# Loading the first half of x in two column parts, in a two-layer encoder kernel on one core

## The chip, the cores and the metric

The kernel runs on one NeuronCore of a Trainium2 chip. The engines are TensorE (PE in the rows; its weight loads are PEld), VectorE (DVE), ScalarE (ACT), GpSimd (POOL) and SyncE (SP), which here only issues DMA transfers. The metric is the device time of one execution in microseconds (us). A lower time is better.

## The reference

The program computes two layers of an encoder over 256 tokens of width 1024, in float32. Cut to what matters:

```
def mixer_sublayer(x, norm_g, w_in, qk_g, rpb, mix_g, w_out):
    h = rms_norm(x, norm_g)
    proj = h @ w_in                                  # 256 x 1024 @ 1024 x 2304
    qa, ka, va, qb, kb, vb, qc, kc, vc = jnp.split(proj, ...)
    ...                                              # three kinds of attention: oa, ob, oc
    merged = jnp.concatenate([rms_norm(oa, ...), rms_norm(ob, ...), rms_norm(oc, ...)], axis=-1)
    return merged @ w_out

for l in range(2):
    x = x + mixer_sublayer(x, norm1_g[l], w_in[l], ...)
    x = x + hier_moe(rms_norm(x, norm2_g[l]), ...)   # 32 experts, two of them per token
```

`rms_norm(x, g)` divides each row of x by the root of its mean square and multiplies by a gain per column.

## The kernel before, in words

Each layer has two stages. In the mixer stage the input projection `w_in` comes in three groups of 768 columns (C, A, B, in this order), and attention is interleaved with them. In the expert stage the 32 experts' weights (6 MB each) stream through a ring of 16 pieces of 1 MB in SBUF, with some further buffers beside it. All engines run a program that is written out by hand: each engine's instructions stand in the order of the code, and engines wait for each other by semaphores only.

The change is at the very start of layer 0. The 256 tokens are two halves of 128 rows (`t` = 0 and 1), which lie in SBUF as `x[:, t]`, 128 partitions of 1024 columns. Every projection needs x turned, with its columns on the partitions. TensorE turns it in blocks of 128 columns: `half_turned(l, t, j)` turns four blocks, columns 512 j to 512 j + 511 of half t, into one PSUM bank. VectorE multiplies these by the gain of `norm1_g` into `hT` (`rows_turned`, line 1439). The projection uses the turned x as its weights (`project`, line 782). The division by the row's root is done later, when VectorE takes a projection out of PSUM (`projected`, line 1453): ScalarE sums the squares (`x_squares` and `mean_squares`, line 1212), GpSimd takes the root (lines 661 and 664).

SyncE's queue starts like this (`mixers`, lines 526 to 557): the identity matrix `ident` (64 KB), x's first half (512 KB, one transfer, semaphore `d_x[0]`), the upper four row blocks of the first 256 columns of group C (512 KB, semaphore `landed`), x's second half (512 KB, `d_x[1]`), the lower four row blocks of these columns (512 KB, `d_lower[0]`), and then the other 512 columns of group C in two transfers of 1 MB. Behind them come the window biases (`in_na_rpb`, `in_c_flip`), the rotary tables (`in_c_rope`), the gains of queries and keys (`in_qk_norm_g`, line 470), a mask, group A (line 562), and so on without a wait until the expert stage's first pieces. Three small transfers of gains (4 KB each) are issued from ScalarE's own queue (line 1308, semaphore `d_gains`).

TensorE starts like this (its `mixers`): it waits for `ident`, runs two warming products of the identity (line 741), waits for the gains and turns them (line 791), and then

```
                if l == 0:
                    half_turned(l, 0, 0)
                half_turned(l, 0, 1)
                project(l, 0)
                project(l, 1)
                project(l, 2)
```

In `project(l, 0)`, between block 3 and block 4, x's second half is turned as well.

Of the kernel before, what the change touches and what calls it, by code (L numbers as in the profile page):

```python
# [163 lines left out]
def encoder(nc, a, out):  # L164
    ctx = ExitStack()
    with ctx:
        def sb(name, shape, dt=F32):
            return ctx.enter_context(nc.sbuf_tensor(name, shape, dt))

        def sem(name):  # L170
            return ctx.enter_context(nc.semaphore(name))
# [3 lines left out]
        x = sb("x", [P, TT, D])  # L175
# [87 lines left out]
        def carve(n):  # L263
# [32 lines left out]


        d_x = [sem(f"d_x{t}") for t in range(TT)]
        d_ident, d_gains, d_rel, d_mask, d_rope, d_qkg, d_route, d_gain2, d_const, d_out = (
            sem("d_" + n) for n in ("ident", "gains", "rel", "mask", "rope", "qkg", "route", "gain2", "const", "out"))  # L300

# [117 lines left out]
        def _(sp):  # L419
            extra = sp.alloc_register("sp_extra")  # L420
            xr = a["x"].rearrange("b (t p) d -> (b p) t d", t=TT)
# [104 lines left out]
            def mixers(l):  # L526
                if l == 0:
                    sp.dma_start(ident[:], a["c_ident"]).then_inc(d_ident, 16)
                    sp.dma_start(x[:, 0], xr[:, 0]).then_inc(d_x[0], 16)
                for g in range(3):  # L530
                    if g == 1:
                        if l == 0:
# [96 lines left out]
            def rerun(l, j, x0):  # L629
# [3 lines left out]
                for r in range(6):  # L633
                    w, k = weight(("w_gate", "w_up", "w_down")[r // 2], l, bass.ds(expert, 1))
                    sp.dma_start(rows(r, k), w[:, 0, r % 2 * k:r % 2 * k + k]).then_inc(d_again, 16)

            run_layers(sp, extra, mixers, first, item, rerun, seen[0])

            outr = out.rearrange("b (t p) d -> (b p) t d", t=TT)
# [93 lines left out]
        def _(pe):  # L733
# [13 lines left out]
            def half_turned(l, t, j):  # L747

                if l == 0:
                    pe.wait_ge(d_x[t], 16)  # L750
                else:
                    pe.wait_ge(v_back[BACK.index((t, j))], l)
                for k in range(4):
                    last = transpose(bank[2 * t + j][:, k * P:k * P + P], x[:, t, (4 * j + k) * P:(4 * j + k + 1) * P], ident[:])
                last.then_inc(p_xT, 1)
# [177 lines left out]
            def mixers(l):  # L933
# [3 lines left out]
                if l == 0:  # L937
                    half_turned(l, 0, 0)
# [265 lines left out]
        def _(act):  # L1204
# [6 lines left out]
            def mean_squares(t, c):  # L1211
                activation(h[:, t * D:t * D + D], x[:, t, :], ACT.Square, scale=D ** -0.5, accum_out=ms[:, c:c + 1]).then_inc(a_ms, 1)  # L1212

            def x_squares(l, t):
                if l == 0:
                    act.wait_ge(d_x[t], 16)
                else:
                    for half in range(2):
                        act.wait_ge(v_back[BACK.index((t, half))], l)
                mean_squares(t, t)  # L1220
# [89 lines left out]
            def mixers(l):  # L1310
                if l == 0:
                    first_loads()
                    act.wait_ge(g_init, 4)
                x_squares(l, 0)
                x_squares(l, 1)

                activation(spare[:], one[:], ACT.Exp)
# [640 lines left out]
```

## Time and profile before

| | us |
|---|---|
| median of 3 runs | 1154.4 |
| lowest and highest of them | 1153.38, 1154.82 |
| the profiled execution | 1152.95 |
| its span, from the first to the last instruction | 1151.1 |
| TensorE busy in it | 981.2 |
| VectorE, ScalarE, GpSimd busy | 291.6, 178.2, 51.6 |
| DMA, over the span | 437.08 MB, mean 380 GB/s |

The profile is of one execution. Its time is the span and 1.85 us around it. All times within it are counted from the start of the span. "SPq" and "ACTq" are the DMA issues of SyncE and ScalarE; the time of an issue is that of issuing alone, and the time to landing is told apart from it.

### The profile page before, as it was taken

How to read it: one execution, taken by the hardware profiler on the slowest of the kernel's cores; microseconds unless marked ns; L12 is line 12 of the kernel's file. 1: busy time of each engine (PE TensorE's matmuls, PEld its weight loads, DVE VectorE, ACT ScalarE, POOL GpSimd, SP SyncE). 2: the span in 40 equal slices, each digit the busy share in tenths (PEclk: the TensorE clock that was granted, in tenths of full speed). 3: DMA queues.
4: the chain of work that ended last, by engine and by line, in shares of the span. 5: the costliest groups of instructions: out<-in, count | busy, mean ns of one | idle time of the engine just before them, and what ended most of it. 6: DMA issues, size and time to landing. Idle time of an engine off the chain costs nothing.

```text
span 1151.1 us, 13649 instructions
## 1 busy us (share of the span) xinstructions
PE 981.2 (85%) x5406; PEld 461.6 (40%) x5406; DVE 291.6 (25%) x796; ACT 178.2 (15%) x444; POOL 51.6 (4%) x104
## 2 busy tenths in 40 slices
PE   8999999998887956548899999999969879484687
PEld 5556644453343412114356656444524334131232
DVE  4546552111110110001145555421111101100011
ACT  1344311110010000002024343111100001000110
POOL 2121100000000000000021211000000000000000
PEclk9999999999898977869999999999989989687899
DMA  9962989999999999999998248999999999999997
GB/s 318 345 259 110 363 317 422 424 427 428 428 428 427 428 430 426 429 428 421 400 396 319 101 178 342 358 419 427 428 428 427 428 428 427 428 427 428 428 420 299
DMA packets 64759, 437.08 MB, mean 380 GB/s; under 512 B 11229, under 2 KB 15669, under 8 KB 34229
## 3 DMA queue, kind: packets, MB, share of 16 engines
q1 hardware_dynamic: 64645, 436.16, 92.4%
q8 instruction: 45, 0.74, 0.3%
q14 instruction: 21, 0.17, 0.0%
q10 hardware_dynamic: 48, 0.01, 0.0%
HBM read 435.10 MB, written 1.44 MB: 379 GB/s over the span
## 4 chain that ended last, share of the span: by engine, by line
PE 63%; DMA 31%; DVE 3%; SPq 1%; issue 1%; POOL 1%; ACT 0%; DVEq 0%; POOLq 0%
PE bank L1071 32%; DMA ring<-in_w_down 16%; DMA ring<-in_w_gate 10%; PE bank L782 9%; DMA ring<-in_w_up 5%; PE bank L1097 5%; PE bank L914 5%; PE bank L1025 4%; PE bank L741 1%; PE bank L860 1%; PE bank L850 1%; SPq L513 1%; PE bank L882 1%; PE bank L1089 1%; PE bank L873 1%
## 5 line engine op out<-in xcount | busy, mean ns | idle before, releaser
L1071 PE MATMUL bank<-ring,work 128*32 128x512 f32 (+2 forms) x2608 | 480.8, 661 | 133.7 <-DMA ring<-in_w_up 50.5
L1071 PEld LDWEIGHTS bank<-ring,work 128*32 128x32 f32 (+2 forms) x2608 | 145.3, 129 | 397.7 <-issue 394.5
L782 PE MATMUL bank<-ring,hT 128*128 128x512 f32 (+1 forms) x384 | 128.3, 488 | 0.9 <-DVE hT L1439 0.8
L782 PEld LDWEIGHTS bank<-ring,hT 128*128 128x128 f32 x384 | 71.2, 190 | 48.1 <-issue 42.2
L1025 PEld LDWEIGHTS bank<-work,h 128*128 128x128 f32 x704 | 82.3, 192 | 16.5 <-issue 15.6
L1025 PE MATMUL bank<-work,h 128*128 128x128 f32 x704 | 86.8, 277 | 1.6 <-DVE work L1804 1.6
L1071 PE MATMUL bank<-work 128*32 128x512 f32 (+2 forms) x176 | 75.1, 617 | 13.8 <-DMA ring<-in_w_down 13.8
L1097 PE MATMUL bank<-work 128*128 128x512 f32 x176 | 81.4, 603 | 2.4 <-ACT work L1392 1.6
L1071 PE MATMUL bank<-kept,work 128*32 128x512 f32 (+1 forms) x160 | 72.6, 606 | 4.2 <-DMA ring<-in_w_up 4.2
L1860 DVE COPY work<-bank 128x512 f32<-128x512 f32 x20 | 13.8, 692 | 243.6 <-PE bank L1071 243.6
L1855 DVE TENSOR_TENSOR work<-work,bank 128x512 f32<-128x512 f32 x22 | 15.1, 688 | 218.3 <-PE bank L1071 218.3
L1826 DVE TENSOR_SCALAR work<-iota,work,rstd 128x128 f32<-128x128 f32 x80 | 22.3, 343 | 185.2 <-PE bank L1119 183.6
L914 PE MATMUL bank<-ring,h 128*128 128x512 f32 x128 | 58.2, 600 | 0.0
L1387 ACT COPY work<-bank 128x512 f32<-128x512 f32 x22 | 12.9, 585 | 269.5 <-PE bank L1144 269.5
L1383 ACT COPY work<-bank 128x256 f32<-128x256 f32 x22 | 8.2, 372 | 297.4 <-PE bank L1119 297.4
L1097 PEld LDWEIGHTS bank<-work 128*128 128x128 f32 x176 | 31.8, 189 | 50.9 <-issue 49.2
L1392 ACT COPY work<-bank 128x512 f32<-128x512 f32 x22 | 12.9, 585 | 170.7 <-PE bank L1071 156.2
L1071 PEld LDWEIGHTS bank<-work 128*32 128x32 f32 (+2 forms) x176 | 21.2, 135 | 39.4 <-issue 39.2
L741 PE MATMUL bank<-ident 128*128 128x384 f32 x86 | 31.8, 514 | 2.8 <-DMA ident<-in_c_ident 2.8
L914 PEld LDWEIGHTS bank<-ring,h 128*128 128x128 f32 x128 | 23.2, 190 | 25.3 <-issue 25.0
L1372 ACT ACTIVATE work<-bank,gain 128x128 f32<-128x128 f32 x88 | 25.1, 368 | 42.1 <-PE bank L1025 42.1
L661 POOL TENSOR_TENSOR ms<-ms,eps 128x1 f32<-128x1 f32 x20 | 3.8, 189 | 552.0 <-ACT h L1212 466.0
(212 smaller groups left out, 716.8 us busy)
## 6 DMA issues: line engine op xcount, KB each, us to landing
ring<-in_w_gate SPq DMA_DIRECT2D x42, 2048.0 KB, 25.1
ring<-in_w_down SPq DMA_DIRECT2D x38, 2048.0 KB, 23.8
ring<-in_w_up SPq DMA_DIRECT2D x36, 2048.0 KB, 30.0
ring<-in_w_up SPq DMA_DIRECT2D x36, 1024.0 KB, 14.7
ring<-in_w_down SPq DMA_DIRECT2D x28, 1024.0 KB, 10.3
ring<-in_w_gate SPq DMA_DIRECT2D x20, 1024.0 KB, 8.1
ring<-in_w_in SPq DMA_DIRECT2D x8, 1536.0 KB, 13.6
ring<-in_w_out SPq DMA_DIRECT2D x8, 1024.0 KB, 17.0
```

What stands on the lines that cost most here:

```text
L741: matmul(bank[b][:, 0:3 * P].rearrange("p (n s) -> p n s", n=3), ident[:], ident[:].unsqueeze(1).broadcast_to([P, 3, P]), start=True, stop ...
L782: last = matmul(bank[6 + i % 2][:, 0:c1 - c0], hT[:, k, t * P:t * P + P], group_in(l, gi)[:, k, c0:c1], start=(k == 0), stop=(k == KD - 1))
L914: last = matmul(bank[6 + n % 2][:, :], mixed[:, pos0 + c, t * P:t * P + P], rows(pos, 2)[:, c % 2, half * 512:half * 512 + 512], start=(c ...
L1025: last = nc.tensor.matmul(bank[banks[k // 4]][:, k % 4 * P:k % 4 * P + P], x_kc[:, t, k, :], pick[:, t, :], start=(t == 0), stop=(t == TT ...
L1071: last = nc.tensor.matmul(bank[b][e * w:e * w + w, :], lhs[:, k, e * w:e * w + w], rows(pos, k_count // 2)[:, kk, n * 512:n * 512 + 512], ...
L1097: last = nc.tensor.matmul(bank[SUM0 + n][:, :], pickT[:, t, :], y[:, half * 512:half * 512 + 512], start=(of == 0), stop=(of == NI - 1))
L1372: last = nc.scalar.mul(xg[:, k, :], bank[pair(i)[1]][:, (k - 4) * P:(k - 3) * P], gain2[:, q // NI, k:k + 1])
L1387: nc.scalar.copy(hidT.rearrange("p c s -> p (c s)"), bank[b0][:, :]).then_inc(a_hidT, 1)
L1392: nc.scalar.copy(y[:, 0:512], bank[b0][:, :]).then_inc(a_y, 1)
L1826: last = ts(hot[:, n], iota[:, 0:P], seats[:, TIME[i], n:n + 1], factors[n], ALU.is_equal, ALU.mult)
L1855: tt(hid, hid, bank[b1][:, :], ALU.mult).then_inc(v_hid, 1)
L1860: nc.vector.tensor_copy(y[:, 512:1024], bank[b1][:, :]).then_inc(v_y, 1)
```

## The change

The load of x's first half becomes two transfers, of columns 0 to 511 and of columns 512 to 1023, each 128 rows of 2 KB (256 KB). The first one raises `d_x[0]`, the second a new semaphore, `d_right`. TensorE's first turn (columns 0 to 511) waits for `d_x[0]`, the second turn for `d_right`. ScalarE, which squares all 1024 columns of the half, waits for both. Nothing else is edited.

```
+        d_right = sem("d_right")
...
                     sp.dma_start(ident[:], a["c_ident"]).then_inc(d_ident, 16)
-                    sp.dma_start(x[:, 0], xr[:, 0]).then_inc(d_x[0], 16)
+                    for j in range(2):
+                        sp.dma_start(x[:, 0, j * 512:j * 512 + 512], xr[:, 0, j * 512:j * 512 + 512]).then_inc((d_x[0], d_right)[j], 16)
...
             def half_turned(l, t, j):
                 if l == 0:
-                    pe.wait_ge(d_x[t], 16)
+                    pe.wait_ge(d_right if (t, j) == (0, 1) else d_x[t], 16)
...
             def x_squares(l, t):
                 if l == 0:
                     act.wait_ge(d_x[t], 16)
+                    if t == 0:
+                        act.wait_ge(d_right, 16)
```

On SyncE, at the start of the program, the queue of transfers before was this:

```order
L528 DMA ident<-in_c_ident 128x128
L529 DMA x<-in_x 128x1024
L555 DMA ring<-in_w_in 128x4x256
L557 DMA x<-in_x 128x1024
L555 DMA ring<-in_w_in 128x4x256
L555 DMA ring<-in_w_in 128x4x512 x2
```

And with the change (the lines are numbered one or two higher):

```order
L529 DMA ident<-in_c_ident 128x128
L531 DMA x<-in_x 128x512 x2
L557 DMA ring<-in_w_in 128x4x256
L559 DMA x<-in_x 128x1024
L557 DMA ring<-in_w_in 128x4x256
L557 DMA ring<-in_w_in 128x4x512 x2
```

Everything behind x's first half stands one issue later; the order is the same.

On TensorE, at the start of the program, with the semaphores it waits for, before:

```order
L741 MATMUL bank<-ident 128x384 [waits d_ident]
L741 MATMUL bank<-ident 128x384
L791 MATMUL bank<-ident,work 128x24 [waits d_gains]
L754 MATMUL bank<-ident,x 128x128 [waits d_x0]
L754 MATMUL bank<-ident,x 128x128 x3
L754 MATMUL bank<-ident,x 128x128 [waits d_x0]
L754 MATMUL bank<-ident,x 128x128 x3
L782 MATMUL bank<-ring,hT 128x256 [waits landed0,v_xT]
```

And with the change:

```order
L743 MATMUL bank<-ident 128x384 [waits d_ident]
L743 MATMUL bank<-ident 128x384
L793 MATMUL bank<-ident,work 128x24 [waits d_gains]
L756 MATMUL bank<-ident,x 128x128 [waits d_x0]
L756 MATMUL bank<-ident,x 128x128 x3
L756 MATMUL bank<-ident,x 128x128 [waits d_right]
L756 MATMUL bank<-ident,x 128x128 x3
L784 MATMUL bank<-ring,hT 128x256 [waits landed0,v_xT]
```

No instruction moved; the fifth turn waits for another semaphore.

## Rows read from the trace of the kernel before

**Rows 1.** Busy us by stretch (PE, PEld, DVE, ACT, POOL), granted clock, DMA share, GB/s
```profile
0.00:30.00 30.00, 27.10 (x99) 16.21 (x100) 12.72 (x29) 5.68 (x10) 7.61 (x23) 1.00 0.93 305
...
86.00:115.00 29.00, 28.21 (x143) 17.58 (x142) 19.55 (x44) 12.15 (x43) 4.42 (x9) 1.00 0.28 109
```

**Rows 2.** Chain of waits, the first 11 us: start, duration, what
```profile
0.78 1.91 DMA ident<-in_c_ident
...
2.80 2.90 PE bank L741 x4
5.70 0.23 PE bank L791
5.93 1.06 PE bank L754 x4
...
7.84 1.99 PE bank L782 x8
9.83 0.87 PE bank L754 x8
```

**Rows 3.** Timeline of TensorE's matmuls and weight loads, three places: start, duration, what
```profile
4.86 0.85 PE L741 MATMUL bank<-ident 128*128 128x384 f32 x1
...
5.63 0.18 PEld L791 LDWEIGHTS bank<-ident,work 24*128 24x128 f32 x1 [1.08 <-DMA work<-in_norm_g]
...
6.77 0.66 PEld L754 LDWEIGHTS bank<-ident,x 128*128 128x128 f32 x3
...
10.44 0.52 PEld L782 LDWEIGHTS bank<-ring,hT 128*128 128x128 f32 x3
```

**Rows 4.** Timeline, SyncE's issues from 1.2 to 2.8 us: start, duration of the issue
```profile
1.22 0.42 SPq L529 DMA_DIRECT2D x<-in_x  x1
1.69 0.43 SPq L555 DMA_DIRECT2D ring<-in_w_in  x1
2.16 0.51 SPq L557 DMA_DIRECT2D x<-in_x  x1
2.71 1.93 SPq L555 DMA_DIRECT2D ring<-in_w_in  x3
```

**Rows 5.** Issues by line, four short windows: KB each, us from issue to landing
```profile
x<-in_x SPq DMA_DIRECT2D x1, 512.0 KB, 4.1
...
ring<-in_w_in SPq DMA_DIRECT2D x1, 512.0 KB, 5.1
...
x<-in_x SPq DMA_DIRECT2D x1, 512.0 KB, 5.9
...
ring<-in_w_in SPq DMA_DIRECT2D x1, 1024.0 KB, 9.1
ring<-in_w_in SPq DMA_DIRECT2D x1, 512.0 KB, 6.9
```

**Rows 6.** DMA packets of 5.0 to 5.2 us, then of 5.6 to 6.0 us
```profile
DMA packets 72, 0.07 MB, mean 369 GB/s; under 512 B 0, under 2 KB 72, under 8 KB 72
...
DMA packets 118, 0.17 MB, mean 420 GB/s; under 512 B 8, under 2 KB 100, under 8 KB 118
```

**Rows 7.** Timeline, 5 to 16 us, of ScalarE, GpSimd and VectorE
```profile
5.40 1.28 ACT L1212 ACT_TABLE_LOAD   x1 [5.40 <-DMA x<-in_x]
...
8.26 0.55 POOL L664 TENSOR_TENSOR rstd<-ms,mhalf 128x1 f32<-128x1 f32 x1
...
12.47 0.48 DVE L1453 TENSOR_SCALAR work<-bank,rstd 128x256 f32<-128x256 f32 x1 [0.88 <-PE bank L782]
...
15.93 0.48 DVE L1453 TENSOR_SCALAR work<-bank,rstd 128x256 f32<-128x256 f32 x1 [2.97 <-PE bank L782]
```

**Rows 8.** Timeline, 18 to 26 us, from the scaled rotary table to the turned keys
```profile
18.63 0.46 POOL L689 TENSOR_TENSOR kept<-kept 128x128 f32<-128x128 f32 x1
...
22.29 0.76 DVE L1498 TENSOR_TENSOR work<-work 128x256 f32<-128x256 f32 x2
...
25.41 0.42 PEld L816 LDWEIGHTS bank<-ident,work 128*128 128x128 f32 x4 [0.60 <-issue]
```

More of the change, by code:

```diff
@@ L298, in encoder @@
         d_x = [sem(f"d_x{t}") for t in range(TT)]
+        d_right = sem("d_right")
         d_ident, d_gains, d_rel, d_mask, d_rope, d_qkg, d_route, d_gain2, d_const, d_out = (
@@ L528, in mixers @@
                     sp.dma_start(ident[:], a["c_ident"]).then_inc(d_ident, 16)
-                    sp.dma_start(x[:, 0], xr[:, 0]).then_inc(d_x[0], 16)
+                    for j in range(2):
+                        sp.dma_start(x[:, 0, j * 512:j * 512 + 512], xr[:, 0, j * 512:j * 512 + 512]).then_inc((d_x[0], d_right)[j], 16)
                 for g in range(3):
@@ L749, in half_turned @@
                 if l == 0:
-                    pe.wait_ge(d_x[t], 16)
+                    pe.wait_ge(d_right if (t, j) == (0, 1) else d_x[t], 16)
                 else:
@@ L1216, in x_squares @@
                     act.wait_ge(d_x[t], 16)
+                    if t == 0:
+                        act.wait_ge(d_right, 16)
                 else:
```

## The prediction

> **What bounds the kernel now.** I read the busy time by stretch first, then the chain of waits, then the timeline of the first 16 us, then how long each transfer took to land.
>
> The busy time by stretch [rows 1] says which engine the start hangs on. Of its first 30 us TensorE is busy for 27.1, and the other 2.9 are the wait at the very start. The reader is to see three more things: the granted clock is 1.00, that is the upper of the two levels (2.4 GHz), the DMA engines are busy for 0.93 of this stretch at 305 GB/s, and later in the same mixer stage, from 86 to 115 us, they are busy for 0.28 only. So the start is a matter of TensorE's path, and a transfer that lands somewhat later has room to be caught up before the expert stage begins. A shift of TensorE at the start would on the other hand be passed on to the end, since TensorE has next to no idle time in the mixer stage.
>
> The chain of waits [rows 2] says what TensorE's path is. `ident` is issued at 0.78 and takes 1.91 us. TensorE then runs the two warming products (four instructions, 2.80 to 5.70), the turn of the gains (5.70), the four turns of x's left half (5.93), and after VectorE's product the projection (7.84). No transfer of x is in the chain. That is the main finding: the first turn does not wait for x.
>
> When does x's first half land? Its issue starts at 1.22 [rows 4] and it takes 4.1 us [rows 5], so it lands at 5.3. ScalarE, which really waits for it, starts its table load at 5.40 [rows 7], which agrees. TensorE cannot start a turn before it has done the warming products and the gains: the last warming instruction starts at 4.86, the gains' weight load at 5.63 [rows 3], the first turn at about 5.9. x has been there for some 0.5 us by then.
>
> **The change part by part.**
>
> The first part alone is waited for. x's left half is 256 KB. It cannot land later than the whole did, as it is the first half of the same bytes on the same queue. Its landing goes from 5.3 to, say, 4.6: the 256 KB saved are 0.6 to 0.7 us at the 369 to 420 GB/s that the DMA engines moved at [rows 6]. TensorE is at 4.6 still in its third or fourth warming instruction. Worth: 0. The upper bound on any gain, if x's landing did gate the turn in executions other than the profiled one, is these 0.7 us.
>
> The second part. It is issued one issue later than the left half, at about 1.22 + 0.42 + 0.05 = 1.69. It moves the second half of the same bytes. Earliest landing 5.3 as before, latest 5.3 and one issue, 0.47 us (the distance of the issues at 1.22 and 1.69 [rows 4]), so 5.8. TensorE wants it for the fifth turn, whose weights load at 6.77 [rows 3]. 1.0 us of slack. Cost 0.
>
> More packets. The half now goes as 256 pieces of 2 KB where it was 128 of 4 KB. The trace shows no 2 KB pieces in this stretch, so I bound them by smaller ones: from 5.0 to 5.2 us all 72 packets are under 2 KB (the weights' rows of 1 KB), at 369 GB/s. From 5.6 to 6.0, with larger ones among them, it is 420 GB/s [rows 6]. 512 KB take 1.42 us at the one rate and 1.25 at the other. So the smaller pieces cost between 0 and 0.17 us. I take 0.1 on the DMA engines, and look below whether anything on the path sees it.
>
> Everything behind on SyncE's queue is issued 0.47 us later. That is one more instruction on a queue that doesn't wait before the expert stage. Each of these transfers lands between 0 later (the DMA engines are the limit from 4 us on, and they have the same bytes to move in the same order) and 0.47 + 0.17 = 0.64 us later. I go through the ones that TensorE's path needs early:
> - The upper blocks of the first 256 columns: issue at 1.69, 5.1 us, landed at 6.8 [rows 4, 5]. Used at 7.84 [rows 2]. Slack 1.0.
> - x's second half: 2.16 + 5.9 = 8.1 [rows 4, 5]. Turned from 9.83 on, in the chain [rows 2]. Slack 1.8 (1.4 by the weight load, which runs ahead).
> - The lower blocks: 2.71 + 6.9 = 9.6 [rows 4, 5]. Used from 10.44 on [rows 3]. Slack 0.8. This is the tightest, and still 0.2 above the worst of the two bounds.
> - The next 512 columns, upper blocks: issued about 0.47 behind, at 3.2, 9.1 us, landed at 12.3 [rows 5]. The second unit of the projection is taken out at 15.93 [rows 7], and only then does the third begin. Slack 3.6.
> - The query and key gains, for GpSimd's rotary products at 18.63 [rows 8]. Here GpSimd may start up to 0.64 later, and VectorE with it. VectorE has the keys ready at 22.29 + 0.76 = 23.05, and TensorE takes them at 25.41, after the bias products. Slack 2.4.
> - All others land farther from their use, and before the expert stage there is the stretch at DMA share 0.28 [rows 1], some 20 us of free DMA time. Cost 0 in each.
>
> ScalarE's second wait. Both squares need all of x's first half. ScalarE waits to 5.3 before and to 5.3 to 5.8 now, then loads the table and squares. What is queued behind it is the square of the second half, and GpSimd's two roots wait for these. The first root is there at 8.26 + 0.55 = 8.8, and its first reader, VectorE, comes at 12.47, released by TensorE [rows 7]. Slack 3.7, against a cost of at most 0.64. The second root is a square and a root behind it, and is read at 15.93. Cost 0.
>
> Sum: 0 on TensorE's path. The profiled execution would stay at 1152.95 us (span 1151.1 and 1.85 around it). The median of the runs shown is 1154.4, 1.45 above it. That is the runs' own scatter (1153.38 to 1154.82), so I forecast the median again: 1154.4 us.
>
> One rule speaks against the change. From issue to landing the two 512 KB transfers of 1.22 and 1.69 took 4.1 and 5.1 us, so they landed 1.5 us apart, and the next two followed after 1.3 and 1.5 us [rows 4, 5]. The Trainium skill, page "DMA: Bandwidth & Descriptors", section "Anatomy of one DMA — SWDGE (gpsimd) path", gives every DMA some 2.0 us of fixed time and then its bytes at 436 GB/s, and the same page's section "Measured (HBM→SBUF, 128 partitions, SWDGE, issued from GpSimd)" asks for transfers of 1 MiB and up. By that a half alone would be an estimated 2.6 us, and if the two halves stood one behind the other, x would be there 2 us later than by one transfer, which would make TensorE wait. The trace does not agree that they stand so: 512 KB every 1.3 to 1.5 us is 350 to 400 GB/s, and leaves no room for 2 us of each.
>
> **The rivals.**
>
> A, slower: the transfers of a queue are served with a cost of each that adds up, and the lower weight blocks come too late. Place: TensorE's weight load at 10.44. Nearest row for such a cost: `ident`, 64 KB, 1.91 us from issue to landing [rows 2]. If the extra transfer adds that whole, the lower blocks land at 9.6 + 1.9 = 11.5, and TensorE stands for 1.1 us. It decides from a delay of 0.8 us on. There is a second price: in its first turns TensorE took 1.06 us for four, in the next ones 0.87 for eight [rows 2], 0.27 against 0.11 each, although the granted clock reads 1.00. It had been idle before 2.80 and ran at the slow rate to about 8. If a stop sends it back to that for as long (5.2 us), it loses half of them, 2.6 us. Together 3.7 us, 1158.1. For it: the slack is the smallest here. Against it: landings 1.3 to 1.5 us apart, and that TensorE also waits for VectorE before 7.84 without a slow stretch after it.
>
> B, a little faster: x does gate the first turn in ordinary executions, or the small gain transfers, which share the DMA engines with x, get through earlier. The first is worth up to 0.7 us as above. For the second, the warming instructions are 0.64 apart, so TensorE could have gone on at 4.86 + 0.64 = 5.50, and the gains' load is at 5.63 [rows 3]: 0.13 us. At best 1153.7. For it: the mark at the gains' load names a transfer. Against it: 0.5 us of slack for x in the trace.
>
> C, a little slower: the delay is 0.8 to 1.2 us somewhere without the slow rate after it; up to 0.4 us, 1154.8.
>
> That the change doesn't do what it says is not a rival: the order of SyncE and the waits of TensorE show it. What fails is its effect.
>
> **How the numbers follow.** A measurement of this kernel can tell 0.2%, 2.3 us, from no change. Forecast, no effect: 0.86. B: 0.05. C: 0.03. A: 0.04. The last 0.02 are for a gain that no row shows. B and C are within 0.2%. The runs' scatter alone (1.44 us over three) can put a kernel with no effect past 0.2% in some 2 of 100 cases to either side, half of which I count to each. So faster 0.03, within 0.2% 0.92, slower 0.05. The range holds the scatter of such medians and bends toward A: 1152.2 to 1157.0.
>
> **What would show it.** Right: SyncE issues two transfers of x of 256 KB at 1.2 and 1.7, and all behind them 0.4 to 0.5 us later. The left half lands near 4.6, and TensorE's gains' load and first turn still start at 5.6 and 5.9. The fifth turn is at 6.8, the projection at 7.8, its second half at 10.4, with no DMA named before it. ScalarE's table load starts at 5.3 to 5.8, and VectorE takes the first unit at 12.5. Wrong: a first turn clearly before 5.8 (B), or idle time of TensorE before 10.4 released by `in_w_in` and slow turns after it (A).

## The result, and the profile after

| | before | after |
|---|---|---|
| median, us (20 runs each) | 1153.74 | 1155.46 |
| lowest and highest | 1152.48, 1154.82 | 1153.25, 1158.55 |
| ratio of the medians of both, 95% interval | | 1.0016, 1.0010 to 1.0022 |
| the profiled execution and its span | 1152.95, 1151.1 | 1155.61, 1153.8 |

The change makes the kernel slower by 1.7 us by the medians. It is a small loss, but its interval excludes no change, and the scatter grew: the highest run is 3.7 us above the highest of before. I had forecast no effect, so the forecast was wrong, although 1155.46 lies in its range. The loss is 0.16%, within the 0.2% that my prediction took for the finest difference that a measurement of this kernel can tell; 20 runs of each kernel told it.

The chain of waits of the changed kernel, which is the counterpart of [rows 2], shows how far TensorE is behind. Columns are start, duration, what; the lines of code are numbered two to four higher.

```profile
0.78 1.97 DMA ident<-in_c_ident
...
2.86 2.90 PE bank L743 x4
...
5.99 1.06 PE bank L756 x4
...
7.89 1.99 PE bank L784 x8
9.89 0.48 PE bank L756 x4
...
10.39 0.70 DVE hT L1443
...
11.21 12.28 PE bank L784 x40
...
34.14 6.87 PE bank L784 x16
```

To 7.89 all is within 0.1 us of before, as forecast: the first turn did not wait for x, and the earlier left part bought nothing. The eight instructions at 7.89 are the first half of the first projection, on the upper blocks. Behind them come the turns of x's second half, and then a group of 40 projection instructions, of which the first need the lower blocks. I use the start of this group below to tell how late TensorE is. It begins at 11.21, where it was 10.71 before. This view cuts overlapping instructions differently in the two kernels; by the weight load at the head of the group the shift is 0.74 us (11.18 against 10.44). The unit at 34.14 was at 33.38 in the same view of before: 0.76 us of shift by then.

What held TensorE shows in the transfers. First SyncE's issues (start, duration), the counterpart of [rows 4]:

```profile
1.22 0.90 SPq L531 DMA_DIRECT2D x<-in_x  x2
2.16 0.45 SPq L557 DMA_DIRECT2D ring<-in_w_in  x1
2.65 0.50 SPq L559 DMA_DIRECT2D x<-in_x  x1
3.20 1.72 SPq L557 DMA_DIRECT2D ring<-in_w_in  x3
```

Then the issues by line in short windows (KB each, us from issue to landing), the counterpart of [rows 5]: x's left part, x's second half, the upper blocks and the lower blocks.

```profile
x<-in_x SPq DMA_DIRECT2D x1, 256.0 KB, 3.0
...
x<-in_x SPq DMA_DIRECT2D x1, 512.0 KB, 7.0
...
ring<-in_w_in SPq DMA_DIRECT2D x1, 512.0 KB, 5.4
...
ring<-in_w_in SPq DMA_DIRECT2D x1, 512.0 KB, 7.9
```

Issue and time to landing add up to the landing: left part 4.2 (x was at 5.3 as a whole), upper blocks 7.6 (6.8 before), x's second half 9.6 (8.1), lower blocks 11.1 (9.6). The issues are 0.47 later, as forecast, but the last two landings are 1.5 later. The lower blocks were wanted at 10.44, and the 40 instructions start just behind their landing. The second half was wanted at 9.46 by the weight load that runs ahead. The rows of the two weight loads, first that of the second half's turns, then that of the group of 40:

```profile
9.70 0.86 PEld L756 LDWEIGHTS bank<-ident,x 128*128 128x128 f32 x8 [0.21 <-DMA x<-in_x]
...
11.18 5.48 PEld L784 LDWEIGHTS bank<-ring,hT 128*128 128x128 f32 x26 [0.63 <-DVE hT L1443]
```

The first row names x, but the turns started only 0.06 us later than before. The second row, and the chain above, put the larger wait of 0.63 down to VectorE's product, which ended at 11.09. The code says otherwise. In `project(0, 0)`, before block 4, TensorE waits for the second product (`x_turned` gives 2) and for `d_lower[0]`. The product that ended at 11.09 is the third one, and both of the first two were done by 8.44. So it was the lower blocks, which landed at 11.1, that held TensorE here; the profile named the neighbour that ended at the same time.

The bytes are the same, but the DMA engines moved fewer of them just behind the landing of x's right part (4.9). The stretches of 5 to 6 and 6 to 7 us, of before:

```profile
5.00:6.00 1.00, 1.00 (x4) 0.32 (x3) 0.03 (x1) 0.60 (x1) 0.00 (x0) 1.00 1.12 400
6.00:7.00 1.00, 1.00 (x6) 1.00 (x7) 0.15 (x1) 0.99 (x2) 0.00 (x0) 1.00 1.04 422
```

and of after:

```profile
5.00:6.00 1.00, 1.00 (x4) 0.26 (x3) 0.00 (x0) 1.00 (x1) 0.00 (x0) 1.00 1.09 270
6.00:7.00 1.00, 1.00 (x6) 1.00 (x7) 0.18 (x1) 0.99 (x2) 0.00 (x0) 1.00 0.71 254
```

The last two columns are the share of the DMA engines' time that they were busy, and GB/s. In these two microseconds some 300 KB less were moved, 0.75 us at 400 GB/s. From 6 to 7 us the engines were busy for 0.71 of their time, so some of them stood idle although more transfers had been issued; in the other three profiles of the change this share is 0.72 to 0.82. Engines that are idle while others still work point at the rest of the delay: the 16 engines no longer finish a transfer together. From 10.0 to 10.5 us before, all packets are the 2 KB ones of the next transfer; after, 87 packets are of that size or larger, while 22 of the lower blocks' 1 KB packets are still on their way (the 23rd is a semaphore's). Before:

```profile
DMA packets 94, 0.19 MB, mean 385 GB/s; under 512 B 0, under 2 KB 0, under 8 KB 94
```

After:

```profile
DMA packets 110, 0.20 MB, mean 401 GB/s; under 512 B 1, under 2 KB 23, under 8 KB 110
```

The profiled span grew by 2.7 us, the start by 0.8. The other 1.9 arose mostly at the router of each layer, where the granted clock fell in this execution and not in that of before. That turned out to be no doing of the change (below).

### The profile page after: what moved, and what is told of

Same layout as the page of the kernel before. It is cut to its first block, busy times and chain, and to the rows that moved or that the text cites. A ratio compares the mean times of both kernels' runs of the same rounds, so it can differ in the third digit from the quotient of the medians.

```text
span 1153.8 us, 13650 instructions
## 1 busy us (share of the span) xinstructions
PE 984.9 (85%) x5406; PEld 462.7 (40%) x5406; DVE 291.4 (25%) x796; ACT 178.3 (15%) x444; POOL 51.7 (4%) x104
## 4 chain that ended last, share of the span: by engine, by line
PE 64%; DMA 31%; DVE 2%; SPq 1%; POOL 1%; issue 1%; ACT 0%; DVEq 0%; POOLq 0%
PE bank L1073 32%; DMA ring<-in_w_down 16%; DMA ring<-in_w_gate 10%; PE bank L784 9%; DMA ring<-in_w_up 5%; PE bank L1099 5%; PE bank L916 5%; PE bank L1027 4%; PE bank L743 2%; PE bank L862 1%; PE bank L852 1%; SPq L514 1%; PE bank L884 1%; PE bank L1091 1%; PE bank L931 1%
## 5 line engine op out<-in xcount | busy, mean ns | idle before, releaser
L1073 PE MATMUL bank<-work 128*32 128x512 f32 (+2 forms) x176 | 76.0, 623 | 12.8 <-DMA ring<-in_w_down 12.8
L743 PE MATMUL bank<-ident 128*128 128x384 f32 x86 | 34.9, 554 | 2.9 <-DMA ident<-in_c_ident 2.9
## 6 DMA issues: line engine op xcount, KB each, us to landing
ring<-in_w_in SPq DMA_DIRECT2D x8, 1536.0 KB, 14.1
```

Of the source, the lines that this page charges most:

```text
L743: matmul(bank[b][:, 0:3 * P].rearrange("p (n s) -> p n s", n=3), ident[:], ident[:].unsqueeze(1).broadcast_to([P, 3, P]), start=True, stop ...
L1073: last = nc.tensor.matmul(bank[b][e * w:e * w + w, :], lhs[:, k, e * w:e * w + w], rows(pos, k_count // 2)[:, kk, n * 512:n * 512 + 512], ...
```

## The experiments

Landings are issue plus time to landing, in us, each from one profile; "40" is the start of the group of 40 projection instructions. The ratio is to the kernel before on the same chip, whose median was 1153.5 for e1 to e4, 1153.6 for e5 to e9 and 1153.7 for e10 to e13. The last four kernels were profiled once and not timed in rounds; these single executions took 1155.28, 1154.47, 1156.52 and 1154.08 us, and one of the kernel before beside them 1155.57.

| kernel | upper | x second | lower | 40 | median | ratio, 95% |
|---|---|---|---|---|---|---|
| before | 6.8 | 8.1 | 9.6 | 10.7 | 1153.74 | |
| after | 7.6 | 9.6 | 11.1 | 11.2 | 1155.46 | 1.0010 to 1.0022 |
| e1_repeat | 8.9 | 10.2 | 11.6 | 14.5 | 1155.85 | 1.0007 to 1.0026 |
| e2_rows | 7.5 | 8.9 | 10.4 | 10.5 | 1153.94 | 0.9995 to 1.0015 |
| e3_shift064 | 6.8 | 8.1 | 9.5 | 11.6 | 1154.87 | 1.0004 to 1.0022 |
| e4_right_act | 6.6 | 8.7 | 9.9 | 14.6 | 1157.38 | 1.0022 to 1.0047 |
| e5_mask_ahead | 7.3 | 8.5 | 10.0 | 11.2 | 1154.13 | 0.9993 to 1.0011 |
| e7_right_behind | 5.9 | 9.1 | 10.5 | 10.6 | 1155.35 | 1.0009 to 1.0027 |
| e8_late_start | 6.7 | 8.0 | 9.5 | 14.1 | 1157.52 | 1.0021 to 1.0047 |
| e9_ident_act | 7.7 | 9.1 | 10.5 | 12.0 | 1155.26 | 1.0008 to 1.0025 |
| e10_both_left | 6.7 | 8.2 | 9.6 | 10.5 | 1155.10 | 1.0001 to 1.0018 |
| e11_second_split | 6.7 | 8.3 | 9.8 | 10.5 | 1153.49 | 0.9993 to 1.0011 |
| e12_all_split | 8.6 | 9.9 | 11.4 | 13.2 | 1154.76 | 1.0002 to 1.0023 |
| e13_less_warm | 6.8 | 8.1 | 9.5 | 11.1 | 1155.18 | 1.0003 to 1.0020 |
| e14_after_again | 7.8 | 9.3 | 10.7 | 12.7 | | |
| e15_before_again | 6.9 | 8.2 | 9.6 | 10.1 | | |
| e16_after_again | 8.6 | 9.9 | 11.4 | 13.0 | | |
| e17_both_left_again | 6.7 | 8.1 | 9.5 | 11.4 | | |

**e1_repeat**, the change again, no edit.

> The changed kernel once more, as it is. Theory: x's second half again lands near 9.6 us (8.1 before) and the lower blocks of the first 256 columns near 11.1 (9.6 before), TensorE's second half of the first projection starts near 11.2 instead of 10.5, so everything behind is 0.7 to 0.8 later; the rest of the loss is the granted clock falling to the lower level for some 3.4 us at the router of a layer (near 140 and 710 us), 0.75 to 1.0 us each time it happens. Time 1.3 to 2.1 us above the kernel before. Rival (the late landings of the one profile were a chance): landings as before, TensorE's start within 0.2 us of before, and the median less than 0.7 us above.

The landings were later still and TensorE lost far more: its chain of waits names the upper blocks. (`x8` at 8.99 is the first half of the first projection, the next `x8` the turns of x's second half.)

```profile
2.16 6.69 DMA ring<-in_w_in
...
8.99 3.75 PE bank L784 x8
12.74 1.71 PE bank L756 x8
14.45 12.39 PE bank L784 x40
```

TensorE had done its turns at 7.7 and stood for 1.26 us, until 8.99. Then eight instructions took 3.75 us (1.99 before) and eight turns 1.71 (0.87 before), so the group of 40 is 3.7 late. The granted clock reads 1.00 in this stretch, as it does at the very start of the kernel before, where the instructions also take about twice as long: the column doesn't show the start. That it is the lower clock level is therefore read from the durations alone. The clock didn't fall at either router, so that part of the expectation failed here; the span is 1155.4 all the same.

**e8_late_start**, the kernel before with that stop put in by hand.

```
+                            if l == i == 0:
+                                pe.wait_ge(d_lower[0], 16)
```

> The kernel before with its loads untouched; TensorE's first projection also waits for the lower blocks (landed at 9.6), so that it stands idle from about 7.4 to 9.6 and nothing else is changed. Theory (a stop at this place costs its own length and then again as much and more, since TensorE runs on at the slow rate for some 4 to 5 us behind it): the eight instructions of the first half projection take 3.4 to 3.8 us instead of 2.0 and the next eight turns 1.5 to 1.7 instead of 0.87; the group of 40 begins at 13.6 to 14.6 instead of 10.7; time 3 to 4.2 us above before. Rival (a stop costs its own length only): the group of 40 begins at 12.5, time 1.8 above.

Its chain of waits:

```profile
9.60 3.19 PE bank L784 x8
12.79 1.33 PE bank L754 x8
14.12 12.05 PE bank L784 x40
```

TensorE starts the projection 1.76 us late and is 3.4 late at the group of 40; the median is 3.9 us up (ratio 1.0034). One of its six runs took 1678.74 us, for a reason that stays open; the median of the other five, 1157.23, is 3.6 us up. So this stop cost its own length and about as much again in slow instructions. The rival, its own length only, is out.

**e3_shift064**, the loads as before and a shift of TensorE alone.

```
                             half_turned(l, 1, 0)
+                            warm(5, 1)
```

> The kernel before, its loads untouched, with one more warming product (two instructions, 384 columns each) between the turns of x's second half: TensorE is shifted by about 0.64 us there and nothing else is changed. Theory (the start's shift is passed on whole, and a shifted TensorE meets the clock's falls at the router differently): start of the 40 projections 0.6 to 0.7 later, the whole 0.6 us above before and in some executions 0.8 to 1.8 more, median 1.2 to 1.9 above. Rival (the clock's falls come from something else in the changed kernel, the DMA): exactly 0.6 above before, no fall at 140 us. Rival 2 (the shift is swallowed later): as before.

The group of 40 was 0.9 later (0.65 for the product, the rest a longer slow stretch), and the ratio of 1.0013 is 1.5 us with an interval of 0.5 to 2.5. The shift is not swallowed. No fall of the clock came at the router in its profile; whether more than 0.9 was lost stays open.

**e15_before_again**, the kernel before, profiled again.

> The kernel before, a second look of its own. Theory: its landings hardly vary: x 5.2 to 5.4, upper blocks 6.7 to 6.9, second half 8.0 to 8.2, lower blocks 9.4 to 9.7 (as in the three kernels of the study that leave its loads alone), group of 40 at 10.5 to 11.2. Rival (the first look was a lucky one): the upper blocks at 7.5 or later.

Its landings are those of the first profile within 0.1 us. In all five profiles of kernels that leave the loads alone (before, e3, e8, e13, e15) the upper blocks land at 6.7 to 6.9. The group of 40 began at 10.1, earlier than the 10.5 to 11.2 I gave, and the transfers have no part in that. Its eight turns of x's first half took 1.09 us, where in other starts, as e14_after_again's, they take 1.97:

```profile
5.71 1.09 PE L754 MATMUL bank<-ident,x 128*128 128x128 f32 x8
```

So the end of the slow rate itself differs between executions. In the kernels whose landings are in step and whose TensorE program is that of before (before, e5, e11, e15) the group of 40 starts anywhere from 10.1 to 11.2.

The clock also fell at the router of both layers, with nothing changed. The stretches of 138 to 142 us, first profile and second (the column behind POOL is the granted clock, 1.2 GHz where it falls):

```profile
138.00:142.00 4.00, 3.52 (x23) 2.31 (x22) 3.36 (x21) 2.58 (x4) 0.00 (x0) 1.00 1.01 418
```

```profile
138.00:142.00 4.00, 4.00 (x15) 2.26 (x15) 2.67 (x18) 1.97 (x3) 0.00 (x0) 0.58 1.01 416
```

In the second the three warming products there take 3.41 us and hold the routing up; each fall cost 0.7 to 1.1 us. e2_rows had both falls too, with no shift of its start. So these falls come and go with the execution, and the 1.9 us by which the one profile of after exceeds its start's shift are not the change's.

**e14_after_again and e16_after_again**, the change profiled twice more.

> The changed kernel, a third look. Two looks so far: upper blocks landed at 7.6 and 8.9, x's second half at 9.6 and 10.3, lower blocks at 11.1 and 11.6; the group of 40 began at 11.2 and 14.5. Theory (its transfers land late by an amount that differs from execution to execution, and TensorE loses little where the upper blocks come before 7.8 and some 4 us where they come after): upper blocks between 7.0 and 9.0, second half at 9.2 or later; group of 40 at 10.9 to 11.4 if the upper blocks are there by 7.9, at 13 or later if they land after 8.3. Rival (late landings are rare and two looks were a chance): landings at 7.3, 8.6 and 10.1.

> The changed kernel, a fourth look, for how its landings scatter. As for the third look.

In e14_after_again TensorE stopped for 0.2 us only, and the slow rate followed all the same:

```profile
2.16 5.60 DMA ring<-in_w_in
...
7.89 3.75 PE bank L784 x8
11.64 1.10 PE bank L756 x8
12.74 12.05 PE bank L784 x40
```

I had given 10.9 to 11.4 for upper blocks that are there by 7.9, so this part of the expectation failed: what the late start costs does not depend on the stop's length alone. In e16_after_again the upper blocks landed at 8.6, TensorE stood for 1.00 us and the group of 40 began at 13.0, as expected for landings behind 8.3. The stretch from the start of the projection to the group of 40 gives the price of the slow instructions alone. It is 2.87 us before, and 4.24, 4.52, 4.52, 4.85 and 5.46 in e16, e8, e12, e14 and e1, so 1.4 to 2.6 us more, and not in the order of the stops (1.00, 2.19, 1.78, 0.18 and 1.26 us). For e8 the stop is the only edit, so it is the cause there. That a stop of 0.18 us alone did it in e14 is argued: the slow rate reached to about 12 us, and in no start without a stop for a transfer farther than about 9.

Four profiles of the change have the group of 40 at 11.2, 12.7, 13.0 and 14.5, mean 12.8; two of before at 10.7 and 10.1, mean 10.4. That is 2.4 us, beside the 1.7 of the medians and the wider scatter. With so few profiles, and a start that moves by itself between 10.1 and 11.2, the two agree in kind and not as a measurement.

**e2_rows**: one more issue, pieces of 4 KB.

```
+                    for j in range(2):
+                        sp.dma_start(x[64 * j:64 * j + 64, 0], xr[64 * j:64 * j + 64, 0]).then_inc(d_x[0], 16)
```

> x's first half in two transfers by rows, 64 rows of 4 KB each; every reader waits for both. One more issue as in the change, but the pieces stay 4 KB and are as many as before (128). If the extra issue alone makes what is behind land late, x's second half lands 0.5 us or more later than 8.1, the lower blocks at 10.4 or later, and the time is 0.2 to 1.7 us above before. If it is the 2 KB pieces (their number or their mixture with others), all lands at most 0.5 us later than before, TensorE's projection goes on at 10.5, and the time is that of before (within 0.3 us).

The upper blocks are issued 0.80 later, x's second half and the lower blocks 0.96 (the two row parts took longer to issue), and they land 0.7 to 0.8 later, x itself at 6.1. The landings are those of my first alternative and the time is that of the second: from issue to landing nothing got longer (5.0, 5.8 and 6.7 us), the lower blocks come just in time at 10.4, and the time is that of before. The extra issue alone does not do it.

**e5_mask_ahead**: one more issue and 128 more pieces, x as before. The mask's line is moved from behind the rotary tables to behind ident.

```
                     sp.dma_start(ident[:], a["c_ident"]).then_inc(d_ident, 16)
+                    sp.dma_start(colmask[:], a["c_colmask"]).then_inc(d_mask, 16)
                     sp.dma_start(x[:, 0], xr[:, 0]).then_inc(d_x[0], 16)
```

> The kernel before, x in one transfer, but the mask (32 KB, 128 pieces of 256 B) is loaded right behind ident instead of later. That is one more issue and 128 more pieces ahead of the rest, as in the change, with almost no bytes and with x still in 4 KB pieces. Theory (the number of pieces ahead on SyncE's queue sets the 16 DMA engines out of step, so that a transfer lands when its last engine is through): x's second half lands 0.8 us or more later than 8.1, the lower blocks at 10.4 or later, and the time is 0.7 to 3 us above before. Rival (the 2 KB pieces of x itself are the cause): everything lands at most 0.6 us later, TensorE goes on at 10.5 to 10.9, time within 0.4 us of before.

From issue to landing the upper blocks, x's second half and the lower blocks take 5.1, 5.9 and 6.8 us, within 0.1 of what they take before [rows 5]:

```profile
ring<-in_w_in SPq DMA_DIRECT2D x1, 512.0 KB, 5.1
x<-in_x SPq DMA_DIRECT2D x1, 512.0 KB, 5.9
...
ring<-in_w_in SPq DMA_DIRECT2D x1, 512.0 KB, 6.8
```

They land 0.4 to 0.5 later, just as my prediction had it for the change. My theory at this point, the number of pieces ahead, fell. The group of 40 begins at 11.2, as late as in the first profile of the change, but with no wait for a transfer: the slow rate lasted into the projection (eight instructions in 2.46 us), and the median is that of before.

**e9_ident_act**: the change with ident issued from ScalarE's queue, so that SyncE's first issues stand where they stood.

```
-                    sp.dma_start(ident[:], a["c_ident"]).then_inc(d_ident, 16)
...
+                act.dma_start(ident[:], a["c_ident"]).then_inc(d_ident, 16)
```

> The change, but ident is issued from ScalarE's queue ahead of the gains. SyncE's queue then has as many issues and pieces ahead of the weights and of x's second half as before the change (left, right, upper blocks against ident, x, upper blocks). Theory (the number of pieces ahead on SyncE's queue): landings in step again, upper blocks by 6.8, x's second half by 8.2, lower blocks by 9.8, no stop of TensorE, time within 0.4 us of before (the gains land some 0.4 us later, which may put the first turn at 6.2). Rival (2 KB pieces of x are the cause): x's second half and the lower blocks land 1 us or more late again, time 0.7 to 3 us above before.

The upper blocks, issued at 1.69 as before, still took 6.0 us instead of 5.1, and the next two 6.9 and 7.8 instead of 5.9 and 6.9. Its start is late by 1.3 for another reason: ident landed only at 4.0, and the projection and the group of 40 are both 1.3 later, so the late transfers held nothing in this profile. The median, 1.6 us up, says nothing about them; only the landings do. So the lateness is neither one of issue time nor of pieces ahead; it goes with x's two parts.

**e4_right_act**: the right part issued from ScalarE's queue.

```
+                act.dma_start(x[:, 0, 512:1024], xt[:, 0, 512:1024]).then_inc(d_right, 16)
```

> The change, but the right part of x's first half is issued from ScalarE's queue behind the three small gain transfers (at about 2.0 us), so that SyncE's queue has as many issues as before and the first part is half as long. If the place in SyncE's queue (issue and pieces ahead of the rest) is the cause, the upper blocks, x's second half and the lower blocks land as before or earlier, TensorE goes on at 10.5, time as before or 0.3 below. If the number of 2 KB pieces is the cause wherever they are queued, they land 1 to 1.5 us later and the time is 0.7 to 1.8 above. The right part itself should land before 6.8, else the fifth turn is late by the rest.

Issued at 2.07, the right part took 6.4 us and landed at 8.5, 1.7 behind its use: TensorE stopped for 1.62 us, the slow rate followed, and this is one of the two slowest kernels. SyncE's own transfers were better (6.6, 8.7, 9.9), not as before. The answer to the question about the queue is blurred by the stop.

**e7_right_behind**: the right part behind the upper blocks.

```
                                 if l == n == half == 0:
+                                    sp.dma_start(x[:, 0, 512:1024], xr[:, 0, 512:1024]).then_inc(d_right, 16)
                                     sp.dma_start(x[:, 1], xr[:, 1]).then_inc(d_x[1], 16)
```

> The change with the right part of x's first half issued behind the upper blocks of the first columns (order: ident, left, upper blocks, right, x's second half). Same pieces, same number of issues. Right part is wanted at 6.8. Theory (pieces ahead of the transfer that lands late): the upper blocks have no more pieces ahead of them than before and land at about 6.8 or earlier, the right part near 7, x's second half is still late (9 or later). TensorE stops for the right part by 0.3 us or more; time 0.5 to 4 us above before. Rival (the change is slow because the right part stands ahead of the weights): time back at that of before.

The upper blocks came at 5.9 and the right part at 6.9, and TensorE did not stop for it, against my expectation. From issue to landing x's second half took 6.4 us (5.9 before) and the lower blocks 7.3 (6.9). The profiled start lost nothing, while the median is 1.7 us up. The rival, time back at that of before, is out; what cost the 1.7 us is not shown by this profile, and that its executions differ like the change's is my guess.

**e10_both_left and e17_both_left_again**: 2 KB pieces, but in transfers of 512 KB, the left columns of both halves and then the right ones; TensorE turns both left quarters first.

```
-                    sp.dma_start(x[:, 0], xr[:, 0]).then_inc(d_x[0], 16)
+                    sp.dma_start(x[:, :, 0:512], xr[:, :, 0:512]).then_inc(d_x[0], 16)
```

> The kernel before with as many transfers of x as before (two of 512 KB) in the same places of the queue, but cut by columns: the left 512 columns of both halves, then the right 512 columns of both; 256 pieces of 2 KB each. TensorE turns in the order of layer 1 (left of both halves, then right of both), so that no turn wants a transfer earlier than before. Theory now (x in 2 KB pieces at the head of the queue sets the DMA engines out of step, whatever the number of transfers): the second x transfer or the lower blocks land 0.8 us or more later than in the kernel before (8.1 and 9.6), time 0.5 to 4 us above before. Rival (one more transfer is needed for it): landings within 0.3 us of before, time within 0.4 us of before or a little below.

> The kernel with the left columns of both halves in one transfer and the right ones in another, a second look. In the first one all landed as in the kernel before (6.7, 8.2, 9.6), though its median is 0.1% above. Theory A (2 KB pieces at the head make landings late in some executions): in this look or the first one at least one of the three is 0.8 us late, here since the first was not. Theory B (two transfers of 2 KB pieces at the head are needed): as in the first look.

In both profiles all landed as before. Yet the median is 1.4 us up, with an interval that just excludes none. The edit also has a price of its own on TensorE: by its order of turns the right quarter of the first half is turned just ahead of the group of 40, and in both profiles TensorE waits there 0.35 us for VectorE's product of it. That this is all of the 1.4 us is not shown, and late landings in executions that were not profiled are not excluded. Pieces of 2 KB alone don't do it in these two profiles.

**e11_second_split**: the first half whole, the second half in two column parts.

```
-                                    sp.dma_start(x[:, 1], xr[:, 1]).then_inc(d_x[1], 16)
+                                    for j in range(2):
+                                        sp.dma_start(x[:, 1, j * 512:j * 512 + 512], xr[:, 1, j * 512:j * 512 + 512]).then_inc(d_x[1], 16)
```

> The kernel before with x's first half in one transfer of 4 KB pieces and the second half in two by columns (2 KB pieces). Theory A (what counts is that the queue's first big transfer is in 2 KB pieces): upper blocks at 6.8, second half by 8.2 to 8.6, lower blocks by 10.1, time within 0.4 us of before. Theory B (2 KB pieces anywhere among the first transfers do it): lower blocks at 10.5 or later, TensorE stops for them, time 0.5 us or more above.

Landings in step, and the time of before, as theory A has it. The same split is harmless one transfer later.

**e12_all_split**: the change, and the second half in two parts as well (the edit of e11_second_split on top of it).

> The change with x's second half in two transfers by columns as well: all of x is in 2 KB pieces and the 4 KB pieces are gone. If the late landings come from 4 KB pieces that follow the 2 KB ones, they go: x's second half by 8.6 to 9, lower blocks by 10.6, time within 0.8 us of before. If they come from the 2 KB pieces at the head, they stay: lower blocks at 11 or later, time 1.5 to 4 us above before.

The upper blocks came at 8.6, TensorE stood for 1.78 us until they were there, and the group of 40 began at 13.2. Its eight turns had been quick (1.09 us), and the eight instructions behind the stop were slow (3.39 us): a stop also takes back a speed that was reached. The median is 1.0 us above before (1.5 by the ratio), below or at the lower end of the 1.5 to 4 that I gave. So the landings are late without any 4 KB pieces behind, too.

**e13_less_warm**: the kernel before with half the warming at the start.

```
-                    warm(6, 2)
+                    warm(6, 1)
```

> The kernel before with one warming product at the start instead of two (1.28 us of TensorE less, ahead of the gains). x is landed at 5.3, so the first turn can start at 5.4 at the earliest instead of 5.9. This is the test of how much there is to gain ahead of the first turn in a kernel with x in one transfer: at most 0.5 us. Theory (the slow rate reaches 5 us into TensorE's work and restarts after a stop): the stop of about 1 us for x makes more of the following instructions slow, and the time is 0 to 2 us above before. Rival: 0.4 us below before.

It gives the bound on what lies ahead of the first turn, and it isn't x's alone:

```profile
1.72 3.54 DMA work<-in_norm_g
...
5.31 0.30 PE bank L791
5.61 1.90 PE bank L754 x8
7.52 2.73 PE bank L782 x8
```

The small gain transfers land at 5.26 and hold TensorE for 1.00 us, until about when x is there. The turns begin 0.3 earlier, but the slow rate reaches farther (the projection's eight instructions take 2.73 us against 1.99), the group of 40 is 0.4 later, and the median is 1.5 us up. Where the other 1.1 us arose is not shown.

No kernel of the study beats the one before.

## Why the prediction was wrong

- **The first part alone is waited for: worth 0.** Right. x's left part lands at 4.2, and the first turn starts at 5.99 (5.93 before).
- **The second part has 1.0 us of slack.** Right; the fifth turn was not held. It landed at about 4.9 (ScalarE, which waits for both parts, began at 4.97), 0.4 before the 5.3 that I had called the earliest.
- **More packets cost 0 to 0.17 us, and everything behind lands 0 to 0.64 later.** This is the step that failed. I had bounded it by the issue's delay plus a rate, taking the 16 DMA engines for one pipe that stays full ("the DMA engines are the limit from 4 us on"). They did not stay full: from 6 to 7 us they were busy for 0.71 of the time and moved 254 GB/s, against 1.04 and 422 before. In four profiles the upper blocks were 0.8 to 2.1 later, x's second half 1.2 to 2.1, the lower blocks 1.1 to 2.0. e5_mask_ahead, to which my bound applies, came out by it: an extra issue and 128 extra pieces, 0.4 to 0.5.
- **The slacks** (1.0, 1.4, 0.8) were read rightly. They were too small for the true delays. The term of my sum, 0 on TensorE's path, came out as a wait of 0.63 us for the lower blocks in the first profile, and as stops of 0.18, 1.00 and 1.26 us for the upper blocks with 1.4 to 2.6 us of slow instructions behind them in the other three. The upper blocks, which I had not called the tightest, did the most harm.
- **ScalarE's second wait: cost 0.** Right for that wait. Its table load even began at 4.97 instead of 5.40, and both roots were there before VectorE wanted them in the first profile.
- **A shift of TensorE's start goes through to the end.** Right. The 0.8 us of the first profile stood unchanged until the router, and e8_late_start's 3.4 us at the group of 40 were 3.4 at its span.
- **Rival A** had the mechanism: transfers late, TensorE stops, then runs slow for a while, together 3.7 us. e1_repeat did just that at the upper blocks, 3.7 at the group of 40. Its reason (a whole fixed cost added per transfer) was wrong, and I gave it 0.04 because the landings of the one profile stood 1.3 to 1.5 us apart. They do, in a kernel whose engines are in step. My argument that TensorE waits before 7.84 "without a slow stretch after it" holds for that wait: in e15_before_again its turns were quick before the same wait of 0.42 us, and no slow stretch followed. It could not speak for others; in e14_after_again one of 0.18 us was followed by a slow stretch.
- **Rival C** (0.03), a delay without the slow rate after it, is what the first profile shows: 0.74 us at the lower blocks. I had priced it at up to 0.4.
- **The forecast's base and its range.** I forecast 1154.4, the median of three runs; the 20 runs of before have 1153.74. The range up to 1157.0, meant for scatter and bent toward A, holds the result; that is no merit of the mechanism I forecast.

The rule of larger transfers that I had set aside (the Trainium skill, page "DMA: Bandwidth & Descriptors", section "Measured (HBM→SBUF, 128 partitions, SWDGE, issued from GpSimd)") pointed the right way here, though e11_second_split went against it and lost nothing. The 2.0 us of fixed time for each transfer (the Trainium skill, same page, section "Anatomy of one DMA — SWDGE (gpsimd) path") are not what was lost: an extra transfer cost 0.4 to 0.5 us in e5_mask_ahead.

Open: why two parts of 256 KB at the head of the queue put the engines out of step. The runs speak against one more issue (e2, e5), more pieces (e5), later issue times (e9), a larger piece behind (e12) and the split one transfer later (e11), each by the landings of one profile, beside all four profiles of the change with late ones. They make 2 KB pieces alone less likely (e10, e17). What is left is two column parts as the first big transfers. The way in which that works is not shown.

## What to carry to other kernels

A transfer's last packets can still be on their way while most of what is moved belongs to the next one, and here that and idle engines made landings 1 to 2 us later than issue times and bytes over bandwidth said. At the start of this kernel slacks under 2 us were none. Before splitting a load, look whether anyone waits for it; here the earlier part was worth nothing from the start, and the delay behind it is the whole effect that the profiles of the change show. A stop of TensorE in its first 10 us cost its own length and 1.4 to 2.6 us of slow instructions on top, with no order by its length (1.00 to 2.19 us, and in one profile 0.18). One profile of each kernel is too few where the start differs from execution to execution.

## What the runs showed of the hardware that was not expected

- The same kernel's transfers landed 1.3 us apart between executions (upper blocks at 7.6, 7.8, 8.6 and 8.9), while before they kept within 0.2.
- With x's first half in two transfers of 256 KB at the head of the queue, the DMA engines moved less, whichever way it was cut: in the stretches 4 to 5 and 5 to 6 us by rows (e2_rows) 231 and 243 GB/s, by columns 305 and 270 in the first profile of the change and 228 and 233 in e1_repeat, against 364 and 400 before. By rows the rate was back at 374 from 6 to 7 us, in the four profiles of the change it was still 216 to 261.
- TensorE's first instructions took about twice as long until some time between 5.7 and 9 us in starts without a stop for a transfer, and until some 11 to 15 us where it stood for 0.18 to 2.19 us between 6.9 and 9.6. The granted clock reads 1.00 throughout.
- The granted clock fell to the lower level at the router (near 139 and 709 us) in some executions of kernels with and without the change (the kernel before: neither in its first profile, both in its second), 0.7 to 1.1 us each.
